# Stick-breaking heads with queries on the partitions, and half-width recurrence levels, in a two-block transformer kernel

## The chip, the core and the metric

The kernel runs on one core of a Trainium2 chip, in one launch. The metric is the device time of an execution in microseconds (us). The median of three runs before the change is 1744.52 us (1741.60 to 1746.47). Engines are written as in the profile: PE (TensorE), DVE (VectorE), ACT (ScalarE), POOL (GpSimd), SP (the engine that issues most DMAs).

## The reference, cut to what matters

512 tokens of width 1024 in fp32 pass through two blocks. The first has a sparse attention, a gating unit and a mixture of experts; the change doesn't touch it. The second puts 16 meta tokens in front of the sequence and mixes it in two ways: eight stick-breaking heads of dimension 64 and four recurrent heads of dimension 128. An output projection and a second mixture of experts follow. The stick-breaking heads compute, for a query t and a key s:

```python
z = jnp.einsum('bhtd,bhsd->bhts', q[:, :, t0:t1], k[:, :, :t1]).astype(jnp.float32) * scale
valid = (s_pos < t_pos) & (s_pos >= LEAD_PAD)
log_beta = jax.nn.log_sigmoid(z)
log_keep = jnp.where(valid, jax.nn.log_sigmoid(-z), 0.0)
log_tail = lax.cumsum(log_keep, axis=3, reverse=True) - log_keep
w = jnp.where(valid, jnp.exp(log_beta + log_tail), 0.0)
outs.append(jnp.einsum('bhts,bhsd->bhtd', w.astype(v.dtype), v[:, :, :t1]))
```

With softplus(z) = max(z, 0) + ln(1 + exp(-|z|)), the weight is exp(z - R), where R is the sum of softplus(z) over the keys from s to t - 1. The recurrent heads, in chunks of 128 tokens, are

```python
bc = jnp.cumsum(gc, axis=2)
diff = bc[:, :, :, None, :] - bc[:, :, None, :, :]
decay = jnp.exp(jnp.where(causal, diff, -jnp.inf))
scores = jnp.einsum('bhtd,bhsd,bhtsd->bhts', qc, kc, decay)
o = jnp.einsum('bhts,bhsv->bhtv', scores, vc) + jnp.einsum('bhtd,bhdv->bhtv', qc * jnp.exp(bc), state)
```

## The kernel before

**The stage.** The work around the change is the mixer loop of the second block: `for i in range(TURNS): for place in range(PLACES):`, written once for each engine. TURNS is 10, PLACES is 4. Turn i starts the scores of stick-breaking head i; the later parts of a head follow in the next turns. From turn 1 to 7 each of the four places also holds one step of the recurrent heads (`step_after`), 28 steps in all, seven levels for each of four heads. Each engine works its own list in order and waits on semaphores for the others; nothing is scheduled at run time. The order is written out by hand.

**A stick-breaking head** keeps keys on the partitions and queries along the row. The five key blocks (one of meta tokens, four of 128 tokens) have 512, 512, 384, 256 and 128 queries, `STICK` = 1792 columns. PE makes the scores z (`scores`, L1961). DVE copies them from PSUM to the buffer `zw` (profile names: arena), scaled and with the causal mask (`stick_scores`, L2721 to L2725). ACT takes |z|, exp(-|z|) and the logarithm into `sps` (ring or misc; L2273, L2275, L2280). DVE adds max(z, 0) (`stick_logits`, L2738, 1792 columns). POOL sums whole blocks of keys (`sums_of_blocks`, L2967, four additions). PE makes the sums R over keys, which lie on the partitions, by products with triangles of ones (`sums_behind`, L1969 and L1972). DVE subtracts them from z (`stick_subtract`, L2734). ACT exponentiates (`stick_weights`, L2284), PE multiplies with the values (`stick_out`, L1982, 14 products), ACT copies the output (L2288), POOL and DVE square, sum and norm it (`head_square` L2952, `head_sums` L2708, `head_norm` L2946, L2947, L2958).

**A recurrence step.** At level lv the queries of the later half of each group of P >> lv tokens meet the keys of the earlier half. POOL makes the differences of decays (`level_diff`, L2982 and L2984), ACT exponentiates (L2294), DVE multiplies queries and keys (`level_products`, L2745 and L2750), PE makes the level's scores (L2012, four products with 128 queries each), and DVE copies them under a mask into `hsc` (`level_read`, L2768, 512 columns). Only the 256 queries of the later halves carry anything.

PSUM has eight banks of 512 fp32 columns. Five go round among the stick-breaking units, three among the recurrent ones (`second_block_units`); PE waits before it fills a bank until its last reader is done. After the loop come the transposes of the mixed rows (`mixed_turned`, L1887), their split in a high and a low part (L2324, L2810) and the output projection (`out_product`, L1727). Its last weight tiles are loaded by SP into the three ring buffers, which lend space to the loop (`sps`, `qexp`, `kd`, `kdR`, `states`).

## Time and profile before

| | us |
|---|---|
| median of 3 runs | 1744.52 |
| profiled execution | 1751.0 |
| its span | 1749.3 |
| PE busy in the span | 1599.1 (91%) |
| DVE | 820.0 (47%) |
| ACT | 335.7 (19%) |
| POOL | 240.2 (14%) |

The profiled execution took 1751.0 us: the span from its first to its last instruction, and 1.7 around it. Busy times are averages over stages of very different kind. In the first block and in both expert stages DVE and POOL are mostly idle; the mixer loop, from about 1027 to 1193 us, is where four engines work at once.

### The profile page before, as it was taken

How to read it: one execution, taken by the hardware profiler on the slowest of the kernel's cores; microseconds unless marked ns; L12 is line 12 of the kernel's file. 1: busy time of each engine (PE TensorE's matmuls, PEld its weight loads, DVE VectorE, ACT ScalarE, POOL GpSimd, SP SyncE). 2: the span in 40 equal slices, each digit the busy share in tenths (PEclk: the TensorE clock that was granted, in tenths of full speed). 3: DMA queues.
4: the chain of work that ended last, by engine and by line, in shares of the span. 5: the costliest groups of instructions: out<-in, count | busy, mean ns of one | idle time of the engine just before them, and what ended most of it. 6: DMA issues, size and time to landing. Idle time of an engine off the chain costs nothing.

```text
span 1749.3 us, 18915 instructions
## 1 busy us (share of the span) xinstructions
PE 1599.1 (91%) x7674; PEld 1027.3 (59%) x7674; DVE 820.0 (47%) x1360; ACT 335.7 (19%) x574; POOL 240.2 (14%) x298
## 2 busy tenths in 40 slices
PE   7999999999999697788699979999699998999996
PEld 5688888877888332333488866778543333333332
DVE  6898645537374410111742358985533322323232
ACT  3422000027101110111311154541200000101011
POOL 1100003300000311100300024781120000000000
PEclk9999999999999899999799988999799999999998
DMA  5122222220237899999322200015899999999993
GB/s 202 49 96 97 74 97 94 97 81 16 101 140 287 331 380 425 428 427 395 156 96 86 90 19 1 1 49 222 312 341 430 430 429 427 430 430 429 430 430 164
DMA packets 52927, 403.26 MB, mean 231 GB/s; under 512 B 13648, under 2 KB 15056, under 8 KB 23776
## 3 DMA queue, kind: packets, MB, share of 16 engines
q1 hardware_dynamic: 45408, 389.34, 55.3%
q0 software_dynamic: 7424, 12.61, 2.1%
q8 instruction: 65, 1.06, 0.2%
q14 instruction: 30, 0.25, 0.0%
HBM read 397.69 MB, written 16.81 MB: 237 GB/s over the span
## 4 chain that ended last, share of the span: by engine, by line
PE 71%; DMA 16%; DVE 6%; issue 3%; ACT 3%; POOL 2%; SPq 0%; POOLq 0%; DVEq 0%; ACTq 0%
PE bank L1727 37%; PE bank L738 14%; DMA arena<-in_expert_in 6%; PE bank L753 6%; PE bank L717 2%; DMA ring<-in_expert_up 2%; DMA arena<-in_expert_up 2%; DMA arena<-in_expert_gate 2%; DMA ring<-in_expert_gate 2%; DMA arena<-in_expert_out 2%; PE bank L916 1%; PE bank L1719 1%; PE bank L718 1%; PE bank L1838 1%; PE bank L1854 1%
## 5 line engine op out<-in xcount | busy, mean ns | idle before, releaser
L738 PE MATMUL bank<-arena 128*64 128x512 f32 x960 | 276.0, 621 | 26.4 <-DMA arena<-in_expert_in 10.7
L738 PE MATMUL bank<-ring,arena 128*64 128x512 f32 x576 | 183.6, 621 | 9.0 <-DMA ring<-in_expert_in 4.7
L738 PEld LDWEIGHTS bank<-arena 128*64 128x64 f32 x960 | 84.1, 142 | 179.2 <-issue 176.7
L1122 DVE TENSOR_TENSOR resid<-resid,bank 128x512 f32<-128x512 f32 x120 | 80.7, 685 | 202.1 <-PE bank L718 202.1
L2411 DVE CAST ring_high<-ring 128x2048 fp32r<-128x2048 f32 x51 | 62.7, 1229 | 236.9 <-DMA ring<-in_stream_a 145.7
L2412 DVE TENSOR_TENSOR ring_low<-ring,ring_high 128x2048 fp32r<-128x2048 f32 x60 | 138.7, 2312 | 6.3 <-ACT ring_high L2083 4.3
L753 PE MATMUL bank<-arena 128*64 128x512 f32 x448 | 114.4, 595 | 13.8 <-DVE arena L1147 6.5
L1727 PE MATMUL bank<-ring_low,xn_high 128*128 128x512 f32 x288 | 113.0, 392 | 0.3 <-DVE ring_low L2412 0.3
L1727 PE MATMUL bank<-ring_high,xn_high 128*128 128x512 f32 x288 | 112.2, 390 | 0.0
L1727 PE MATMUL bank<-ring_high,xn_low 128*128 128x512 f32 x288 | 112.1, 389 | 0.0
L738 PEld LDWEIGHTS bank<-ring,arena 128*64 128x64 f32 x576 | 55.6, 142 | 66.7 <-issue 66.7
L1143 DVE TENSOR_TENSOR arena<-misc,bank 128x256 f32<-128x256 f32 (+1 forms) x32 | 17.6, 551 | 158.8 <-ACT misc L1028 135.6
L1229 POOL DMA_INDIRECT arena<-xn_rows,token_table x32 | 32.6, 1019 | 416.7 <-PE bank L916 379.6
L753 PE MATMUL bank<-ring,arena 128*64 128x512 f32 x288 | 78.6, 596 | 7.1 <-issue 3.7
L753 PEld LDWEIGHTS bank<-arena 128*64 128x64 f32 x448 | 39.4, 137 | 75.5 <-issue 73.1
L1727 PE MATMUL bank<-xn_low,ring_high 128*128 128x512 f32 x192 | 75.0, 391 | 2.4 <-DVE misc L2547 2.4
L1727 PE MATMUL bank<-xn_high,ring_high 128*128 128x512 f32 x192 | 74.8, 389 | 0.0
L1727 PE MATMUL bank<-xn_high,ring_low 128*128 128x512 f32 x192 | 74.7, 389 | 0.0
L1028 ACT ACTIVATE misc<-bank 128x256 f32<-128x256 f32 (+1 forms) x32 | 15.7, 490 | 294.5 <-PE bank L738 294.5
L1261 POOL TENSOR_SCALAR rstd<-ssq 128x1 f32<-128x1 f32 x25 | 11.0, 442 | 422.0 <-ACT arena L1351 258.9
L1114 DVE SCALAR_TENSOR_TENSOR y_low<-bank,gate_slot,y_high 128x512 fp32r<-128x512 f32 x32 | 24.0, 751 | 91.9 <-ACT y_high L1042 91.9
L717 PEld LDWEIGHTS bank<-y_high,spread 128*128 128x128 f32 x128 | 24.0, 187 | 71.9 <-issue 69.2
(393 smaller groups left out, 3052.9 us busy)
## 6 DMA issues: line engine op xcount, KB each, us to landing
ring<-in_stream_a SPq DMA_DIRECT2D x42, 1024.0 KB, 5.0
arena<-in_expert_gate SPq DMA_DIRECT2D x20, 2048.0 KB, 23.0
arena<-in_expert_in SPq DMA_DIRECT2D x18, 2048.0 KB, 33.8
arena<-in_expert_up SPq DMA_DIRECT2D x18, 2048.0 KB, 24.3
arena<-in_expert_down SPq DMA_DIRECT2D x18, 2048.0 KB, 24.5
ring<-in_expert_up SPq DMA_DIRECT2D x12, 2048.0 KB, 25.1
ring<-in_expert_down SPq DMA_DIRECT2D x12, 2048.0 KB, 24.7
ring<-in_expert_gate SPq DMA_DIRECT2D x12, 2048.0 KB, 24.2
```

The costliest lines, as they stand in the source:

```text
L717: nc.tensor.matmul(bank[bank_at][:, :], w, half_of(y_high[:, p % 2, :], half), start=first, stop=False)
L718: ins = nc.tensor.matmul(bank[bank_at][:, :], w, half_of(y_low[p % 2], half), start=False, stop=last)
L738: last = nc.tensor.matmul(h[side * SLOTS:(side + 1) * SLOTS, :], tokens[:, k, side * SLOTS:(side + 1) * SLOTS], w[:, k * 512:(k + 1) * 512 ...
L753: last = nc.tensor.matmul(bank[6 + n][side * SLOTS:(side + 1) * SLOTS, :], hidden[:, f, side * SLOTS:(side + 1) * SLOTS], w[:, f * D + n * ...
L916: last = nc.tensor.transpose(bank[k // 4][:, k % 4 * P:(k % 4 + 1) * P], m.xg[:, p % XG, k * P:(k + 1) * P], c("ident"))
L1114: V.scalar_tensor_tensor(half_of(y_low[p % 2], half), bank[6 + half][:, :], gate_slot[:, p:p + 1], half_of(y_high[:, p % 2, :], half).bitc ...
L1122: nc.vector.tensor_tensor(place, place, bank[bank_at][:, :], ALU.add).then_inc(m.moe_added, 1)
L1143: V.tensor_tensor(m.act[:, 0:m.width], m.sg[:, 0:m.width], up_of(m), ALU.mult).then_inc(m.act_ready, 1)
L1229: G.indirect_dma_start(m.xg[:, p % XG, :], None, m.xn_rows[:, :], bass.IndirectOffsetOnAxis(ap=m.token_table[:, p:p + 1], axis=0), bounds_ ...
L1727: ins = nc.tensor.matmul(b, left(k)[l_], right(k)[r_], start=(first and k == 0 and i == 0), stop=(last and k == KC // 2 - 1 and i == 2))
L2411: then(V.tensor_copy(hi, ring_raw[n % RING]))
L2412: V.tensor_tensor(lo, ring_raw[n % RING], hi.bitcast(F32), ALU.subtract).then_inc(weights_split, 1)
```

## The change

Queries move to the partitions, keys along the row. A head has, for each query block t, the 128 keys of its own block (four pieces, 512 columns) and the rest in front of it: 16 meta keys and t whole blocks, `REST_W` = 16, 144, 272, 400 columns. `STICK` falls from 1792 to 1344, as 112 padding rows of the meta block are gone. The sums R now run along a row, so DVE makes them with eight reversed scans (`stick_sums`): four over the own blocks, which start at zero, then four over the rests, which start from the result of the own block. The scan adds both ln(1 + exp(-|z|)) and max(z, 0), which ACT writes to `above_zero` (a fourth pass, Relu). POOL makes z - R in one subtraction (`exponents`). PE transposes it in 14 pieces, ACT exponentiates from PSUM into `w_turned`, and PE multiplies with the values as before, the meta part with 16 rows. ACT copies the rest's scores out of PSUM, DVE the own blocks' with the mask.

The loop has 9 turns instead of 10. Head i's scans stand at place 2 of turn i, its subtraction at place 3, its transposes at place 1 of the next turn, exponentials at 2, outputs at 3. At each level, the 256 queries are written side by side; PE takes 64 of them in a product, and DVE copies 256 columns. `w_turned` lies in ring buffer 1, so SP's last but one half tile waits for the last output. The turn order of the transposes at the end is new.

```diff
-    put("strict", np.where(row < col, 0.0, NEG))
+    put("strict", np.where(col < row, 0.0, NEG))
@@ sizes
-FIRST_T = [max(s, 1) - 1 for s in range(NT2)]
-STICK_W = [SEQ - P * f for f in FIRST_T]
+REST_W = [META + t * P for t in range(NT)]
+REST_AT = [SEQ + sum(REST_W[:t]) for t in range(NT)]
+STICK = SEQ + sum(REST_W)
+SCORE_UNITS = ((), (0, 1, 2), (3,))
+TURNED_UNITS = (((0, 0), (0, 1), (0, 2), (0, 3)), ((1, 1), (1, 2), (1, 3), (3, 3)), ((2, 2), (2, 3)))
-TURNS = SBH + 2
+TURNS = SBH + 1
-TURN_ORDER = (4, 5, 6, 7, 0, 1, 2, 3)
+TURN_ORDER = (4, 5, 0, 1, 2, 6, 7, 3)
@@ buffers and SP
-        zw = [at(arena, i * STICK, [STICK]) for i in range(3)]
+        zw = [at(arena, i * STICK, [STICK]) for i in (2, 3)]
+        above_zero = at(arena, STICK, [STICK])
+        w_turned = at(ring[1], 0, [TURNED])
-                    sp.wait_ge(psum_filled2, U2.filled(("R", SBH - 2, NT2 - 1)))
+                    sp.wait_ge(psum_filled2, U2.filled(("WT", SBH - 2, 3)))
+                if n == first + 2 * len(STREAM2) - 2:
+                    sp.wait_ge(psum_filled2, U2.filled(("SO", SBH - 1)))
@@ PE
-            def sums_behind(g, blocks):
-                pe.wait_ge(sums_ready, g + 1)
...
+            def exponents_turned(g):
+                pe.wait_ge(exponents_ready, g + 1)
+                e = zw[g % 2]
+                for j, unit in enumerate(TURNED_UNITS):
+                    b = begin2(("WT", g, j))
+                    for n, (s, t) in enumerate(unit):
+                        a = t * P if s == t else REST_AT[t] + META + s * P
+                        last_ = nc.tensor.transpose(b[:, n * P:(n + 1) * P], e[:, a:a + P], c("ident"))
+                    end2(last_)
...
-                    last_ = nc.tensor.matmul(b[:, t * P:(t + 1) * P], keys_,
-                                             qE[:, n % 2, t * P:(t + 1) * P], start=True, stop=True)
+                    last_ = nc.tensor.matmul(b[:, t * P // 2:(t + 1) * P // 2], keys_,
+                                             qE[:, n % 2, t * P // 2:(t + 1) * P // 2], start=True, stop=True)
...
-                    if sums_blocks(i, place):
-                        sums_behind(i - 1, sums_blocks(i, place))
-                    if place == 2 and i >= 2:
-                        stick_out(i - 2)
+                    if place == 3 and i >= 1:
+                        stick_out(i - 1)
                     if step_after(i, place) is not None:
                         step(step_after(i, place))
+                    if place == 1 and i >= 1:
+                        exponents_turned(i - 1)
@@ ACT
+            def stick_scores(h):
+                if h >= 2:
+                    act.wait_ge(psum_filled2, U2.filled(("WT", h - 2, 3)))
+                for j in (1, 2):
...
+                    read2(A.activation(zw[h % 2][:, a:end], b[:, 0:end - a], ACT.Copy, scale=SBD ** -0.5))
...
+                A.activation(above_zero, zw[h % 2], ACT.Relu).then_inc(log_ready, 1)
                 act.wait_ge(act_step, 2 * h + 2)
                 A.activation(v, v, ACT.Ln, bias=1.0).then_inc(log_ready, 1)
...
             def stick_weights(g):
-                wait_read2(act, ("R", g, NT2 - 1))
-                A.activation(zw[g % 3], zw[g % 3], ACT.Exp).then_inc(weight_ready, 1)
+                for j, unit in enumerate(TURNED_UNITS):
+                    b, w = unit2(("WT", g, j)), P * len(unit)
+                    read2(A.activation(w_turned[:, SEQ * j:SEQ * j + w], b[:, 0:w], ACT.Exp))
+                b = unit2(("WT", g, 3))
+                read2(A.activation(w_turned[0:META, META_AT:META_AT + SEQ], b[0:META, :], ACT.Exp))
@@ DVE
+            def sums_from_last(v, a, w, initial):
+                part = v[:, a:a + w][:, ::-1]
+                return V.tensor_tensor_scan(part, part, above_zero[:, a:a + w][:, ::-1], initial, ALU.add, ALU.add)
+            def stick_sums(h):
+                v = sps[h % 2]
+                dve.wait_ge(log_ready, 2 * h + 2)
+                for t in range(NT):
+                    ins = sums_from_last(v, t * P, P, 0.0)
+                then(ins)
+                for t in range(NT):
+                    ins = sums_from_last(v, REST_AT[t], REST_W[t], v[:, t * P:t * P + 1])
+                ins.then_inc(sums_ready, 1)
...
-                read_state(V.copy_predicated(s, level_mask(lv).bitcast(U32),
-                                             b[:, :].rearrange("p (t q) -> p t q", q=P)))
+                read_state(V.copy_predicated(later_queries(hsc[:, h % 2, :], lv), later_mask(lv).bitcast(U32),
+                                             compact_level(b[:, 0:SEQ // 2], lv)))
@@ POOL
-            def sums_of_blocks(g):
...
+            def exponents(g):
+                pool.wait_ge(sums_ready, g + 1)
+                G.tensor_tensor(zw[g % 2], zw[g % 2], sps[g % 2], ALU.subtract).then_inc(exponents_ready, 1)
```

**How the order moves.** PE in turn 6, from the step that follows its scores, before (L1969 and L1972 are the block sums, L1887 and L2005 open a recurrent head, L2012 is a level product, L1982 the outputs of a head):

```order
L2012 MATMUL bank<-resid,arena 128x128 x4
L1969 MATMUL bank<-misc,cst 128x512
L1972 MATMUL bank<-misc,cst 128x512
L1969 MATMUL bank<-misc,cst 128x512
L1972 MATMUL bank<-misc,cst 128x384
L1887 MATMUL bank<-cst,ring 128x128 x4
L2005 MATMUL bank<-arena 128x128 x4
L2012 MATMUL bank<-resid 128x128 x4
L1982 MATMUL bank<-arena 128x64 x14
L2012 MATMUL bank<-resid 128x128 x4
```

The same place after (L2029 is the level product, L1983 and L1987 the transposes):

```order
L2029 MATMUL bank<-resid,arena 128x64 x4
L1889 MATMUL bank<-cst,ring 128x128 x4
L2022 MATMUL bank<-arena 128x128 x4
L2029 MATMUL bank<-resid 128x64 x4
L1983 MATMUL bank<-cst,arena 128x128 x10
L1987 MATMUL bank<-cst,arena 16x128 x4
L2029 MATMUL bank<-resid 128x64 x4
```

Block sums no longer stand between the level products; transposes stand there, and the outputs move one place back.

DVE at place 2 of a turn, before (L2738 is the addition of max(z, 0)):

```order
L2745 TENSOR_TENSOR resid<-resid,arena 128x4x64
L2750 TENSOR_TENSOR resid<-resid,arena 128x4x64
L2768 COPY_PREDICATED resid<-cst,bank 128x512
L2738 SCALAR_TENSOR_TENSOR ring<-arena,ring 128x1792
L2745 TENSOR_TENSOR resid<-resid,arena 128x8x32
L2750 TENSOR_TENSOR resid<-resid,arena 128x8x32
```

And after (L2758 are the scans, listed under the name that the build gives them):

```order
L2775 TENSOR_TENSOR resid<-resid,arena 128x256
L2780 TENSOR_TENSOR resid<-resid,arena 128x4x64
L2811 COPY_PREDICATED resid<-cst,bank 128x256
L2758 SCALAR_TENSOR_TENSOR ring<-ring,arena 128x128 x4
L2758 SCALAR_TENSOR_TENSOR ring<-ring,arena 128x16
L2758 SCALAR_TENSOR_TENSOR ring<-ring,arena 128x144
L2758 SCALAR_TENSOR_TENSOR ring<-ring,arena 128x272
L2758 SCALAR_TENSOR_TENSOR ring<-ring,arena 128x400
L2775 TENSOR_TENSOR resid<-resid,arena 128x256
L2780 TENSOR_TENSOR resid<-resid,arena 128x8x32
```

Eight scans stand in the place of one addition, in front of the next step's products.

## Rows read from the trace of the kernel before

**Rows 1.** Windows: length, then busy of PE, PEld, DVE, ACT, POOL; clock; DMA.

```profile
1026.90:1192.60 165.70, 149.69 (x845) 115.24 (x845) 140.03 (x266) 90.37 (x114) 105.27 (x131) 0.92 0.07 26
...
1103.90:1165.20 61.30, 60.25 (x359) 46.62 (x359) 55.91 (x106) 32.65 (x40) 52.91 (x64) 1.00 0.00 1
...
1192.60:1237.00 44.40, 44.40 (x199) 36.74 (x200) 20.83 (x22) 4.76 (x9) 2.85 (x7) 1.00 0.60 241
```

**Rows 2.** PE timeline at the turns and the end: start, length, instruction.

```profile
1060.64 3.31 PE L1961 MATMUL bank<-arena 64*128 64x512 f32 x10
...
1080.97 6.34 PE L1961 MATMUL bank<-arena 64*128 64x512 f32 x10
...
1103.87 3.28 PE L1961 MATMUL bank<-arena 64*128 64x512 f32 x10
...
1173.98 1.06 PE L2012 MATMUL bank<-resid,arena 128*128 128x128 f32 x8
...
1192.58 0.50 PE L1727 MATMUL bank<-ring_low,state_high 128*128 128x512 f32 x1 [0.52 <-DVE state_low L2810]
```

**Rows 3.** DVE and POOL timelines where they meet, and five scans alone.

```profile
1045.87 3.63 DVE L2702 TENSOR_TENSOR_SCAN arena<-cst,arena 128x128 f32<-128x128 f32 x5
...
1043.61 3.86 POOL L2967 TENSOR_TENSOR ring<-ring 128x128 f32<-128x128 f32 x4 [3.41 <-DVE ring L2738]
...
1056.12 2.02 DVE L2738 SCALAR_TENSOR_TENSOR misc<-arena,misc 128x1792 f32<-128x1792 f32 x1
...
1056.21 2.41 POOL L2984 TENSOR_TENSOR resid<-arena 128x256 f32<-128x256 f32 x1
...
1090.12 1.69 DVE L2702 TENSOR_TENSOR_SCAN arena<-cst,arena 128x128 f32<-128x128 f32 x5
```

**Rows 4.** Groups of instructions: busy us, mean ns; idle before, releaser.

```profile
L2768 DVE COPY_PREDICATED resid<-cst,bank 128x512 f32<-128x512 uint32 x28 | 20.4, 730 | 0.9 <-PE bank L2012 0.8
...
L2734 DVE TENSOR_TENSOR arena<-arena,bank 128x512 f32<-128x512 f32 (+3 forms) x40 | 19.5, 523 | 8.9 <-PE bank L1972 8.0 <-DVE resid L2768 0.3 <-PE bank L1961 0.2
...
L2284 ACT ACTIVATE arena<-arena 128x1792 f32<-128x1792 f32 x8 | 13.5, 1686 | 8.7 <-DVE arena L2734 8.7
...
L2967 POOL TENSOR_TENSOR misc<-misc 128x512 f32<-128x512 f32 x4 | 5.1, 1270 | 0.3
...
L3000 POOL TENSOR_TENSOR arena<-arena 128x512 f32<-128x512 f32 x3 | 4.5, 1491 | 0.2
```

**Rows 5.** PE timeline in turn 4, and transposes at the end.

```profile
1108.07 1.02 PE L1969 MATMUL bank<-misc,cst 128*128 128x512 f32 x2
...
1111.29 1.05 PE L2012 MATMUL bank<-resid,arena 128*128 128x128 f32 x8
1112.18 3.24 PE L1982 MATMUL bank<-arena 128*128 128x64 f32 x28
...
1118.06 0.81 PE L1969 MATMUL bank<-misc,cst 128*128 128x384 f32 x2
...
1190.15 1.92 PE L1887 MATMUL bank<-cst,arena 128*128 128x128 f32 x16
```

**Rows 6.** DVE and POOL timelines of turn 5: free instructions.

```profile
1134.53 0.42 DVE L2745 TENSOR_TENSOR resid<-resid,arena 128x256 f32<-128x256 f32 x1
1134.86 0.42 DVE L2750 TENSOR_TENSOR resid<-resid,arena 128x256 f32<-128x256 f32 x1
...
1135.36 0.61 POOL L2982 TENSOR_TENSOR resid<-arena 128x256 f32<-128x256 f32 x1 [4.36 <-DVE resid L2750]
...
1139.91 3.75 POOL L2967 TENSOR_TENSOR misc<-misc 128x128 f32<-128x128 f32 x4
```

**Rows 7.** Windows around a fall of PE's clock, columns as in rows 1.

```profile
1076.00:1080.00 4.00, 1.65 (x14) 1.48 (x14) 3.85 (x6) 0.58 (x1) 3.77 (x4) 1.00 0.00 0
1080.00:1084.00 4.00, 4.00 (x12) 2.32 (x13) 3.93 (x8) 2.22 (x2) 3.43 (x6) 0.62 0.00 0
1084.00:1088.00 4.00, 4.00 (x10) 2.46 (x10) 2.92 (x9) 0.27 (x1) 0.00 (x0) 0.50 0.00 0
```

220 lines of the change are left out of this document (108 added, 112 removed).

## The prediction

> **What bounds the kernel now.** I read the windows first, to find the stage that the diff touches, then the PE timeline for the rhythm of that stage, then DVE and POOL side by side at the places where an instruction took longer than its shape asks for.
>
> The change lives in the mixer loop of the second block. It runs from PE's scores of head 0 at 1026.9 us to the start of the output projection at 1192.58 [rows 1, 2]. That is 165.7 us of a span of 1749.3; in it PE is busy 149.7, DVE 140.0, POOL 105.3 and ACT 90.4 us [rows 1]. Nothing in front of the loop changes in length. Behind it the projection runs at 44.4 busy of 44.4 us [rows 1], and the expert stage starts from it, so I let a gain or a loss of the loop pass to the end one to one.
>
> Turns are marked by PE's score products: turns 2, 3 and 4 start at 1060.64, 1080.97 and 1103.87, and the last level product, the end of turn 7, begins at 1173.98 [rows 2] and takes 0.89. From 1103.87 to 1174.87 four turns take 71.0 us, 17.75 each. In 1103.9 to 1165.2 PE is busy 60.25 of 61.30, DVE 55.91 and POOL 52.91 [rows 1]. So PE is full, but two engines stand close behind, and they aren't independent. POOL's 256-wide subtraction takes 0.61 us when free (L2982) [rows 6] and 2.41 beside DVE's 2.02 us L2738 (L2984); it ends at 1058.62, 0.5 after DVE's [rows 3]. The five scans L2702 take 1.69 us alone and 3.63 beside POOL's adds L2967 [rows 3]. DVE instructions with two operands in SBUF and POOL's instructions exclude each other. DVE work on a PSUM operand does not: L2768 averages 730 ns over all 28 [rows 4]. I call what the two engines share "the pair". The Trainium skill, SBUF — State Buffer, "Who interferes with whom", states this as an exclusive lock, and the trace agrees. That rule speaks against this change: sums that leave PE land where two engines already wait for each other.
>
> **PE, part by part.** The four block sums from 1108.07 to 1111.29 have 1920 moving columns in 3.22 us, 1.68 ns a column, so a product with 512 advances PE by 0.86 us, one with 128 columns by 0.2225 (four L2012 from 1111.29 to 1112.18, 0.89) [rows 5]. Removed per head: the block sums L1969 and L1972, 3072 columns in nine products, 5.2 us: the four above and five more from 1118.06, at least 1.9 in proportion and 2.0 with the small ones at 0.22 [rows 5]. The scores take 3.2 now (3.28 with the drain) [rows 2]; after, four of 128 columns (0.89) and four of 16, 144, 272 and 400 columns (0.22 + 0.24 + 0.45 + 0.67 = 1.58), 2.47. Added: 14 transposes; 16 took 1.92 us [rows 5], so 1.6. The output products stay 14, at 3.1 (28 records, 3.24 with the drain) [rows 5]. Net 4.3 us per head, 35 in all.
>
> The level products go from 128 to 64 moving columns with the same 128-column weights. L1982 has just that shape: 28 records, 14 products, in 3.1 us, 0.22 each against 0.2225 [rows 5]. I count nothing. The Trainium skill, TensorE: Matmul & The Clock Gate, "Back-to-back issue gap", gives an isolated gap of the columns over 2.4 GHz plus 2.5 ns, by which 112 products would shed about half, some 12 us; the same section notes that the spacing of a load and product pair is set by both, and the row sides with that.
>
> **DVE.** Removed per head: L2738 (2.02), five subtractions (19.5 us over eight heads, 2.4 each [rows 4]) and seven of eight score copies, which read PSUM. Added: one score copy of 512 and eight scans over 1344 columns. A free scan of 128 takes 1.69 / 5 = 0.34 [rows 3]; in proportion 1344 take 3.55, and part of the 0.34 is paid per instruction, so the four long ones are cheaper: 3.4. The copies under a mask, 28 of 512 columns at 0.73 [rows 4], go to 256: about 0.5, 6 us in all. All of this but L2738 and the scans is outside the pair.
>
> **The pair.** Here little is removed. Before, per head: L2738 1.95 and four adds on POOL, 3.75 from first to last [rows 6], together 5.7. After: scans 3.4 and one POOL subtraction of 1344. POOL's add of 512 takes 1.27 [rows 4]; in proportion 1344 take 3.3, with a fixed part less; the slowest row, L3000 with 1.49 [rows 4], gives 3.9, and 2.6 is the low end (1.0 for 512). I take 3.0. Together 6.4, 0.7 more. The rest of the pair in a mean turn: 7.4 level differences on POOL at 0.6 = 4.4 [rows 6]; square and norm of a stick head 1.2; three passes of 512 for three heads over seven turns, 1.4; 7.4 level products on DVE, which start 0.33 apart [rows 6] = 2.5; L2789 and L2791, 512 columns each, 0.6 for half a head. That is 10.1, so 15.8 before and 16.5 after, against a turn of 17.75. Today PE's 17.4 (98%) is longest; after, PE needs 13.1 and the pair 16.5 plus hand-overs, for each waits in order behind the other. If the 1.95 us that a turn lasts beyond the pair's 15.8 stayed, a turn would be 18.4; if they vanished, 16.5. I take 17.8, no change, and keep -1.2 to +0.7 per turn over seven turns, -8 to +5 us.
>
> ACT gets longer but has room: 32.65 busy of 61.30 [rows 1]. Passes of 1792 (1.69, L2284 [rows 4]) become 1.3 at 1344, four instead of three; two score copies of about 0.5 and four weight exponentials read from PSUM, some 2.0, against one of 1.69. About +1.7 per turn. Its chain is hidden as long as the logarithms are done before DVE reaches the scans, two places later; if that cover is gone, a turn is late by what is missing, up to 1.3. Queued behind a scan that waits is DVE's next level product, and PE's level behind that; queued behind the 1344-wide subtraction is the next level difference, then ACT's exponential.
>
> **Slow stretch.** Before the clock fell at 1080.9, PE was busy 1.65 of 4.00 us; it then ran at the half-rate level, 0.62 and 0.50 in the next two stretches, at full busy [rows 7]. That turn took 22.9 (1080.97 to 1103.87) where the turn before, with the same scans L2702, took 20.3 [rows 2]: 2.6 to 3.4 us too many. After, PE's 13.1 us plus some 5 for such a stretch is 18, inside that turn, so the stretch no longer costs: -3. But PE will idle a quarter of each turn and the clock will fall more often; where it falls, each level product is 0.9 us later in DVE's chain. I charge +1 in all, net -2.
>
> **The end.** From the last level product's end to the projection: 1174.87 to 1192.58 = 17.7 us [rows 2]. In it stand head 7's block sums, subtraction, one 1.7 us exponential, the outputs of two heads (3.07 each) and 16 transposes on PE. After, one turn is gone and two heads' outputs become one: POOL's norm of the last but one state head (two passes like L3000 and a root, 3.7) and subtraction (3.0), 1.6 transposes, 2.0 exponentials, 3.07 outputs, copy and square 1.1, low part 0.75, some 15.2 from the last DVE product, which lies about 1 us before that end: 14.2. -3.5, bounds -6 and 0. SP loads the third of the last four half tiles now behind head 7's output instead of earlier. The projection needs it half of 44.4 us after its start, so it stays hidden; were it late, every us counts.
>
> Turns 0 and 1: a longer first ACT chain against cheaper sums: 0, bounds +-3.
>
> **Sum.** 0 - 2 - 3.5 = -5.5. The profiled execution took 1751.0 (span 1749.3 and 1.7 around) and would take 1745.5. It lies 6.5 above the median 1744.5, so on that scale the change gives 1739.
>
> **Rivals.**
> A, PE alone is the bound, and what DVE and POOL lose to each other hides behind it. For it: PE 98% busy. A turn falls to PE's 13.1 at about 92% busy, 14.3, so 3.4 us less in each of seven turns, 24, and little at the end: 1720. Against: rows 3, and POOL busy 52.91 of 61.30 [rows 1]. Chance 0.16.
> B, slower through the clock. The same loop with PE at the half-rate level needs 2 x 13.1 = 26.2 us of PE in a turn. If a stretch like rows 7 comes in each turn, and the levels wait for PE there, each turn loses about 2 us: +14 less 3.5 at the end, 1755; if it stayed low, +60. It decides from the point at which slow stretches fill more than about 40% of the loop. For it: 1.65 of 4.00 us busy sufficed. Against: outputs and scores fill most gaps. Chance 0.16.
> C, the scans or the subtraction dearer (columns read backwards; an initial value from SBUF): every 1 ns a column is 1.3 us of the pair per head, +11 in all, 1750. Chance 0.10.
> D, my case, 0.58.
> The Trainium skill, DVE: opcode table, instruction layouts, handler registers and perf-mode slots, "Datapath and trigger behaviour", says that the built-in scan runs at half throughput. The trace agrees: 2.6 ns a column for 128 against 1.13 in L2738 [rows 3].
>
> **Numbers.** What this kernel's measurement can tell from no change is 0.3%, 5.2 us. D spans 1729 to 1749: 0.30 faster, 0.25 same, 0.03 slower. A is faster. B gives 0.15 slower, 0.01 same. C 0.06 slower, 0.04 same. Together faster 0.46, same 0.30, slower 0.24. Range 1724 to 1757.
>
> **What would show it.** Right: turns of 17 to 18.5 us with PE busy about three quarters; POOL's 1344-wide subtraction at 2.6 to 3.3 us and scans of 3.4 per head, both longer where they meet; 14 us from the last level product to the projection; level products still 0.22 us apart. Wrong: turns under 16 us (A); the granted clock low in over 40% of the loop and PE busy again (B); free scans over 0.45 us for 128 columns (C); a wait of the projection for a weight tile.

## The result, and the profile after

The changed kernel takes 1778.09 us (median of 4 runs, 1773.32 to 1778.46) against 1743.33 of the kernel before on the same chip: ratio 1.0178, 95% interval [1.0152, 1.0205]. That is slower; the forecast was 1739, range 1724 to 1757. The profiled execution has a span of 1776.7 us against 1749.3. The profiled execution of the kernel before (1751.0 us) lies 7.7 above its median, so the traces can account for 27.4 of the 34.8 us between the medians.

The windows of the mixer loop (scores of head 0 to projection, whole), of two stretches in it and of its end; columns as in [rows 1]:

```profile
1028.91:1219.48 190.57, 161.25 (x861) 143.16 (x860) 121.42 (x228) 100.00 (x162) 93.83 (x107) 0.69 0.03 8
1106.00:1121.60 15.60, 15.60 (x63) 13.76 (x63) 6.38 (x12) 6.45 (x9) 7.36 (x11) 0.50 0.00 0
1149.10:1169.40 20.30, 20.30 (x83) 17.99 (x83) 8.59 (x17) 7.99 (x11) 12.65 (x16) 0.50 0.00 1
1203.70:1219.48 15.78, 13.30 (x88) 11.30 (x87) 9.55 (x15) 7.10 (x13) 5.38 (x8) 0.82 0.09 24
```

The loop takes 190.6 us against 165.7 [rows 1]. DVE and POOL did shrink (DVE 121.4 for 140.0, POOL 93.8 for 105.3), yet PE is busy 161.3 us for 149.7, with less work. The reason stands in the third column from the end: the mean granted clock of the loop is 0.69, not 0.92. Since the clock has only two levels (0.50 is 1.2 GHz, 1.00 is 2.4), 62% of the loop ran at the low one (2 x 0.31), against 16% before. In the second and third row PE is busy all through, at 0.50.

The PE timeline at the turns (score products of heads 2 and 7, the last level product, the projection), as [rows 2]:

```profile
1063.46 5.16 PE L1963 MATMUL bank<-arena 64*128 64x128 f32 x16
...
1181.88 5.22 PE L1963 MATMUL bank<-arena 64*128 64x128 f32 x16
...
1201.96 1.97 PE L2029 MATMUL bank<-resid,arena 128*128 128x64 f32 x8
...
1219.48 0.79 PE L1729 MATMUL bank<-ring_low,state_high 128*128 128x512 f32 x1 [1.56 <-DVE state_low L2853]
```

From the start of turn 2 to the end of the last level product: 1063.46 to 1203.7, 140.3 us; before, 1060.64 to 1174.87, 114.2 [rows 2]. The six turns went from 19.0 to 23.4 us each and carry nearly the whole loss, 26.0. Turns 0 and 1 take 34.5 for 33.8 us, the end 15.8 for 17.7, and the loop starts 2.1 us later. 26.0 + 0.7 - 1.9 + 2.1 = 26.9 of the 27.4 us between the spans.

How PE runs in such a turn: the output stage (L1997 with 128 rows, L1999 with 16) at either clock, and the wait ahead of it:

```profile
1058.29 0.33 PE L1997 MATMUL bank<-arena,ring 128*128 128x64 f32 x2
1058.55 0.43 PE L1999 MATMUL bank<-arena,ring 16*128 16x64 f32 x2
1058.91 0.66 PE L1997 MATMUL bank<-arena,ring 128*128 128x64 f32 x4
...
1062.43 1.10 PE L2029 MATMUL bank<-resid 128*128 128x64 f32 x8
...
1076.96 0.49 PE L1997 MATMUL bank<-arena,ring 128*128 128x64 f32 x2 [1.53 <-ACT ring L2317]
1077.37 0.68 PE L1999 MATMUL bank<-arena,ring 16*128 16x64 f32 x2
...
1084.25 1.11 PE L1889 MATMUL bank<-cst,ring 128*128 128x128 f32 x4
...
1101.62 0.69 PE L1997 MATMUL bank<-arena,ring 128*128 128x64 f32 x2 [3.76 <-ACT ring L2317]
```

(Two records are one fp32 product.) At the full clock the stage takes 1058.29 to 1062.43, 4.14 us, not the 3.07 of the same 14 products before: a 16-row product (1058.55 to 1058.91) advances PE by 0.36 us where a 128-row one takes 0.22, and the two 128-row products behind it take 0.59 (1058.91 to 1059.50), not 0.44. So it is the change between the two kinds that costs, some 0.15 us each (an estimate: 1.07 us over seven changes). At the low clock the stage is 7.29 us (1076.96 to 1084.25). The scores take 5.2 us at the low clock, in the turns shown above, and 2.7 at the full one (1088.08 to 1090.76, for 2.47 in the forecast).

What came before the clock fell: windows around three falls in the changed kernel, to set beside [rows 7], columns as in [rows 1]:

```profile
1060.10:1063.50 3.40, 3.40 (x27) 3.07 (x26) 3.12 (x9) 1.08 (x3) 1.97 (x3) 1.00 0.00 0
1063.60:1067.00 3.40, 3.40 (x14) 3.25 (x15) 3.37 (x4) 0.00 (x0) 2.70 (x3) 0.50 0.00 0
...
1125.00:1128.40 3.40, 3.40 (x25) 3.00 (x25) 3.33 (x7) 0.70 (x2) 1.15 (x2) 1.00 0.02 5
1128.40:1131.80 3.40, 3.40 (x16) 3.17 (x16) 3.40 (x2) 0.37 (x1) 3.25 (x2) 0.50 0.00 0
...
1172.80:1176.10 3.30, 3.30 (x25) 2.90 (x23) 2.91 (x6) 1.11 (x2) 1.98 (x3) 1.00 0.00 0
1176.20:1179.60 3.40, 3.40 (x17) 3.17 (x15) 0.00 (x0) 0.90 (x2) 3.40 (x3) 0.50 0.02 5
```

Each time PE was busy all through a stretch at 1.00, and the next was granted 0.50. What stood ahead of these falls were, for the most part, the 64-column and 16-row products of the output stage. But they are not the rule. The record of the clock has ten falls in this loop; the 3.4 us ahead of the other seven:

```profile
1032.85:1036.25 3.40, 0.29 (x1) 0.00 (x0) 3.29 (x7) 3.31 (x5) 2.52 (x4) 1.00 0.00 0
1049.92:1053.32 3.40, 1.92 (x18) 1.78 (x18) 3.34 (x4) 2.68 (x5) 3.40 (x5) 1.00 0.00 0
1073.81:1077.21 3.40, 1.87 (x17) 1.66 (x15) 2.57 (x8) 3.40 (x7) 2.67 (x5) 1.00 0.02 5
1097.70:1101.10 3.40, 0.16 (x2) 0.02 (x1) 3.21 (x9) 3.40 (x10) 2.59 (x4) 1.00 0.00 0
1142.08:1145.48 3.40, 1.12 (x9) 0.97 (x8) 2.31 (x5) 3.40 (x5) 0.89 (x3) 1.00 0.00 0
1193.28:1196.68 3.40, 2.36 (x18) 2.08 (x16) 3.25 (x6) 2.10 (x6) 3.19 (x3) 1.00 0.60 176
1213.76:1217.16 3.40, 3.40 (x25) 3.00 (x25) 2.96 (x5) 0.14 (x2) 1.80 (x2) 1.00 0.00 0
```

Six of the ten came while PE idled for part of the time, as in [rows 7], where it was busy 1.65 of 4.00 us. The low stretches behind these six add up to 81.9 us, the two longest (20.5 and 23.9 us) among them; those behind the four fully busy ones to 36.4 us of the loop. So both roads lead down. Once the clock was low, PE busy all through did not bring it back for 15.6 and 20.3 us (the first rows of this section). The kernel before has two falls in its loop and 27.3 us at the low clock, against 118.4.

The groups that answer to [rows 4], within the loop and by shape:

```profile
L1999 PE MATMUL bank<-arena,ring 16*128 16x64 f32 x64 | 18.1, 374 | 0.0
...
L2811 DVE COPY_PREDICATED resid<-cst,bank 128x256 f32<-128x256 uint32 x28 | 14.6, 520 | 35.2 <-PE bank L2029 35.1
...
L3005 POOL TENSOR_TENSOR arena<-arena,ring 128x1344 f32<-128x1344 f32 x4 | 14.3, 3576 | 9.6 <-DVE ring L2758 9.6
...
L3005 POOL TENSOR_TENSOR arena<-arena,misc 128x1344 f32<-128x1344 f32 x4 | 12.6, 3140 | 2.2 <-DVE misc L2758 2.2
```

The first head's eight scans on the DVE timeline, which answer to the five of [rows 3]:

```profile
1042.69 3.69 DVE L2758 TENSOR_TENSOR_SCAN ring<-ring,arena 128x128 f32<-128x128 f32 x8 [5.76 <-ACT ring L2310]
```

The copy under the mask has fallen from 730 to 520 ns, but DVE waited 35.1 us for PE's level products ahead of it; before, such waits came to 0.8 [rows 4]. DVE waits for PE now.

### The profile page after: what moved, and what is told of

Same layout as the page of the kernel before. It is cut to its first block, busy times and chain, and to the rows that moved or that the text cites. A ratio compares the mean times of both kernels' runs of the same rounds, so it can differ in the third digit from the quotient of the medians.

```text
span 1776.7 us, 18931 instructions
## 1 busy us (share of the span) xinstructions
PE 1614.4 (91%) x7690; PEld 1054.9 (59%) x7690; DVE 799.2 (45%) x1320; ACT 344.8 (19%) x622; POOL 228.5 (13%) x274
## 4 chain that ended last, share of the span: by engine, by line
PE 77%; DMA 12%; ACT 4%; DVE 3%; issue 2%; POOL 1%; SPq 0%; POOLq 0%; ACTq 0%; DVEq 0%
PE bank L1729 38%; PE bank L736 15%; PE bank L751 7%; DMA arena<-in_expert_in 6%; PE bank L715 2%; PE bank L1997 2%; DMA ring<-in_expert_up 2%; DMA arena<-in_expert_up 2%; DMA arena<-in_expert_out 2%; PE bank L1963 1%; PE bank L914 1%; PE bank L716 1%; PE bank L1721 1%; PE bank L2029 1%; PE bank L1840 1%
## 5 line engine op out<-in xcount | busy, mean ns | idle before, releaser
L1120 DVE TENSOR_TENSOR resid<-resid,bank 128x512 f32<-128x512 f32 x120 | 80.7, 685 | 199.8 <-PE bank L716 199.8
## 6 DMA issues: line engine op xcount, KB each, us to landing
arena<-in_expert_in SPq DMA_DIRECT2D x18, 2048.0 KB, 33.8
ring<-in_expert_up SPq DMA_DIRECT2D x12, 2048.0 KB, 23.4
```

Source lines behind the costliest of these rows:

```text
L1120: nc.vector.tensor_tensor(place, place, bank[bank_at][:, :], ALU.add).then_inc(m.moe_added, 1)
```

## The experiments

The theories: 1, the granted clock falls because wide products were taken out and narrow ones left (1b: because TensorE idles, whatever the width of its products); 2, the chain through VectorE, GpSimd and ScalarE is itself longer and the clock only goes along; 3, the switches between 128-row and 16-row products make TensorE the bound; 4, the order ties TensorE and ScalarE into a cycle.

Eighteen kernels were run. "Loop" is the profiled execution's time from the first scores to the projection, "clock" the mean granted clock in it, "PE" its busy time there; loop, clock and PE are each of one execution. Each ratio is taken against executions of the kernel before in the same round, whose median went from 1743.3 to 1747.0.

| kernel | median us | ratio to before [95%] | loop us | clock | PE us |
|---|---|---|---|---|---|
| before | 1743.3 | | 165.8 | 0.92 | 149.8 |
| changed | 1778.1 | 1.0178 [1.0152, 1.0205] | 190.6 | 0.69 | 161.3 |
| half_levels_alone | 1748.4 | 1.0017 [1.0001, 1.0033] | 164.5 | 0.92 | 149.0 |
| full_levels | 1774.6 | 1.0176 [1.0158, 1.0195] | 190.7 | 0.71 | 158.0 |
| sums_cut | (below) | | 163.5 | 0.77 | 138.5 |
| filler | 1786.0 | 1.0235 [1.0212, 1.0257] | 199.8 | 0.85 | 183.0 |
| wide_columns | 1769.3 | 1.0152 [1.0133, 1.0172] | 184.2 | 0.78 | 149.2 |
| wide_filled | 1760.4 | 1.0075 [1.0048, 1.0103] | 176.4 | 0.88 | 149.1 |
| outputs_later | 1798.8 | 1.0318 [1.0276, 1.0359] | 212.4 | 0.63 | 176.6 |
| meta_paired | 1762.2 | 1.0121 [1.0064, 1.0177] | 178.4 | 0.73 | 147.8 |
| scores_ahead | 1775.6 | 1.0190 [1.0155, 1.0225] | 189.1 | 0.68 | 163.3 |
| ahead_paired | 1768.1 | 1.0144 [1.0107, 1.0182] | 181.4 | 0.71 | 154.1 |
| ahead_wide_paired | 1758.6 | 1.0067 [1.0035, 1.0098] | 174.2 | 0.80 | 139.2 |
| ahead_wide_paired_filled | 1748.8 | 1.0025 [0.9999, 1.0051] | 166.7 | 0.89 | 136.5 |
| filled_narrow | 1754.9 | 1.0063 [1.0041, 1.0084] | 174.1 | 0.86 | 142.4 |
| wide_paired_filled | 1749.4 | 1.0031 [1.0012, 1.0050] | 163.7 | 0.92 | 132.0 |
| ahead_filled_start | 1756.3 | 1.0069 [1.0048, 1.0091] | 175.9 | 0.88 | 155.7 |
| before_start_filled | 1747.2 | 1.0013 [0.9995, 1.0031] | 165.4 | 0.95 | 156.3 |
| rows_full | 1757.4 | 1.0058 [1.0033, 1.0082] | 171.3 | 0.74 | 140.2 |
| rows_wide_filled | 1740.6 | 0.9966 [0.9952, 0.9981] | 158.0 | 0.92 | 124.0 |

### Which part of the change: half_levels_alone, full_levels

```
half_levels_alone, on the kernel before (also the compact copy under the mask):
-  matmul(b[:, t*P:(t+1)*P], keys_, qE[:, n%2, t*P:(t+1)*P])
+  matmul(b[:, t*P//2:(t+1)*P//2], keys_, qE[:, n%2, t*P//2:(t+1)*P//2])
full_levels: the reverse of it, on the changed kernel
```

> The kernel before with only the second part of the change: levels multiply and copy the later halves' 256 queries. Theory 1 (clock): the block sums' wide products are still there, so the clock stays as before, and the shorter predicated copies give back 0 to 5 us: 1738-1745; if the 64-column level products alone were what lowers the clock, 1755 or more. Theory 2: 1736-1742.

> The changed kernel with one of its two parts taken back: recurrence levels multiply and copy all 512 queries again. Theory 1 (clock): 128 columns in place of 64 in 112 products raise TensorE's activity a little, and the predicated copy costs 28 x 0.3 us on VectorE: 1765-1785. Theory 2: the copies only add to VectorE, 1783-1790.

Alone, the half-width levels measured 1.0017 [1.0001, 1.0033], no gain: DVE's busy time in the loop fell by 4.3 us and the loop by 1.3. Taken back from the changed kernel they moved nothing either (1.0176 against 1.0178). Neither run finds the loss in the half-width levels, so it is that of the rebuilt stick heads.

### Are the removed wide products what held the clock: sums_cut

```
on the kernel before, for each of 5 blocks:
-  matmul(b[:, 0:w], tri_ge, sps[:, a:a+w]); matmul(b[:, w-behind:w], tri_lt, sps[:, a+w:a+w+behind])
+  matmul(b[:, 0:64], tri_ge, sps[:, a:a+64])
-  zs - b[:, 0:w]
+  zs - b[:, 0:64] broadcast to w
```

> The kernel before with its block sums on TensorE cut from 9 wide products to 5 of 64 columns for each head (work left out: only the first 64 columns of each block are summed, VectorE subtracts these for the whole block at the same width, so its instructions keep their size). Some 4.2 us of TensorE work less in each turn, nothing else changed. Theory 1 (clock: the wide products kept the granted clock up): low time in the loop rises from 27 us to 60 or more, and the time does not fall by more than 5 us, more likely rises: 1740-1765. Theory 2 (chain): the clock doesn't matter, TensorE was not the bound: 1735-1743, turns of 17-18 us as before.

Its whole time (2136.1 us) can't be compared, for with other numbers out of the mixer the expert stage behind it has other work; the loop can. There some 33 us of PE work at the full clock (5.2 less 5 x 0.22 for each of 8 heads) are gone, and no work of the other engines with it; the granted clock fell from 0.92 to 0.77 (75 us low for 27) and the loop from 165.8 only to 163.5. This is the change's first step by itself. In its profiled execution every one of its six falls came behind a stretch in which PE idled (busy 0.00 to 2.70 of 3.4 us): with the sums gone PE had more to wait for, and that brings the clock down without any new narrow products. How much the low clock took back isn't shown: a turn of this kernel with the clock at 1.00 all through (1076.41 to 1093.81) took 17.4 us, near the 17.75 of before, with DVE busy 16.8 of it, which suggests that the other engines would have kept most of the gain in any case.

### Width and filling: filler, wide_columns, wide_filled

```
filler, ahead of each of 28 waits for level_ready (56 products):
+  matmul(b[:, :], ident, sbq[:, 0, :]) x2
wide_columns:
-  matmul(b[:, t*64:(t+1)*64], ..., sbv[:, s+1, g*64:(g+1)*64])
+  matmul(b[:, t*128:(t+1)*128], ..., sbv[:, s+1, g//2*128:(g//2+1)*128])    (copy takes 64 of 128)
-  matmul(b[:, t*64:t*64+64], keys_, qE[..., t*64:t*64+64])
+  wide = 128 if t < 3 else 64; matmul(b[:, t*64:t*64+wide], keys_, qE[..., t*64:t*64+wide])
wide_filled: wide_columns, 2 extra products at the outputs' wait, 1 at every third level's
```

> The changed kernel with two extra products of 512 columns (unused, overwritten by the level product behind them) placed ahead of each of the 28 waits for a level's operands, 56 in all. Theory 1 (the clock): the loop is long because TensorE is granted the low level for over half of it; work put where it only waited keeps the granted clock up, turns shrink from 22.5-24.5 us to 18-19, and the time falls from 1778 to 1735-1750 although work was added. Theory 2 (the chain through VectorE, GpSimd and ScalarE is itself longer, and the low clock only goes along with the waits): the clock may rise, the turns stay at 22-24 us, and the time stays at 1775-1790.

> The changed kernel with the moving side of its narrow products made 128 columns: all 14 output products of a stick head (the neighbour head's 64 columns are computed too and not copied), and three of four in each level product (the next tile's 64 columns, written over by the next product). No product more, none less; by the rows of before 64 and 128 columns take about the same 0.22 us. Theory 1 (clock, and it is the narrow products that don't hold it): fewer low stretches, 1745-1765. Theory 1b (clock, but idle TensorE lowers it, whatever the width): no change, 1770-1780, low stretches as before. Theory 2 (longer chain on the other engines): no change, 1775-1780.

> The kernel with 128-column output and level products (wide_columns) with 21 extra products of 512 columns, only where TensorE was seen to wait: two ahead of the wait for each head's turned weights (heads 0 to 6), one ahead of the level product at the third place of each of 7 turns. That is 18 us of work at the full clock. Theory 1 (clock): 56 extra products were too many (TensorE was busy 183 of 200 us); 21 keep the clock and fit into the idle 35 us of wide_columns: low time in the loop from 82 to under 40 us, loop from 184 to 165-175 us, 1748-1760. Theory 2 (chain through the other engines): the loop stays at 182-190, 1767-1775.

The filler raised the clock to 0.85, as the clock theory says, but did not lower the time: 48 us of extra work went onto a PE that then was busy 183 of 200 us. My number for it was wrong, as 56 products don't fit the waits, and its 1786 us lies in the range of theory 2, so this run does not decide. Of its eight falls seven came with PE busy 3.29 to 3.40 of the 3.4 us ahead: with the waits filled, the falls behind idle PE are nearly gone, those behind busy PE are not.

Widening adds no product; the clock went to 0.78, PE's busy time from 161.3 to 149.2 and the loop from 190.6 to 184.2. Its five falls all came behind idle PE:

```profile
1030.57:1033.97 3.40, 0.36 (x2) 0.00 (x0) 3.29 (x7) 3.31 (x5) 2.45 (x4) 1.00 0.00 0
1068.12:1071.52 3.40, 1.67 (x14) 1.20 (x11) 2.62 (x8) 3.40 (x5) 1.97 (x4) 1.00 0.02 5
1095.42:1098.82 3.40, 0.00 (x0) 0.00 (x0) 3.37 (x8) 3.40 (x9) 2.22 (x4) 1.00 0.00 0
1136.38:1139.78 3.40, 1.23 (x12) 0.88 (x10) 2.70 (x8) 3.40 (x9) 0.00 (x0) 1.00 0.00 0
1184.17:1187.57 3.40, 1.29 (x8) 1.05 (x8) 3.29 (x6) 2.06 (x6) 3.15 (x3) 1.00 0.41 173
```

It isn't free: at the full clock the output stage takes 4.67 us (1055.82 to 1060.49 in its PE timeline) for 4.14. Its 1769.3 us lies between the two forecasts (1745 to 1765, and 1770 to 1780), and its ratio (1.0152) overlaps the changed kernel's interval; with 21 fillers it is apart from it: 1.0075 [1.0048, 1.0103], clock 0.88. That speaks against theory 2, which had 1767 to 1775. The forecasts of theory 1 (loop 165 to 175, 1748 to 1760) were just missed.

### The order of outputs and scores: outputs_later, scores_ahead, ahead_paired, ahead_wide_paired, ahead_wide_paired_filled, wide_paired_filled

```
outputs_later:  stick_out(i-1) behind step() at place 3, not ahead of it
scores_ahead:   -  place 0: scores(i)
                +  place 3 of turn i-1: scores(i), ahead of stick_out(i-2); ScalarE's score copies with it
*_paired:       the 16-row product comes first in tiles 1 and 3, last in tiles 0 and 2
*_wide:         as wide_columns;   *_filled: 1 extra product at the outputs' wait and at every third level
```

> The changed kernel with one swap in the order: the output products of a stick head stand behind the level product at the fourth place of a turn, not ahead of it. Theory 1 (clock): TensorE waits 2.5-3.8 us less for ScalarE's exponentials in each turn, but the level product then waits as long for its own operands; the low stretches remain, 1770-1778. Theory 2 (the wait for the turned weights sits in the loop's cycle): the levels no longer stand behind it, turns shorten by 1-2 us, 1763-1770.

> The changed kernel with the score products of the next stick head (and ScalarE's copies of them) moved from the start of a turn to the fourth place of the turn before, ahead of the output products. Theory 4 (a cycle between two engines): in the changed kernel the next scores stand behind the outputs on TensorE, the outputs wait for ScalarE's exponentials of the turned logits, and these stand behind ScalarE's passes over the current scores; the path is about 10.1 us of ScalarE plus 8.5 us of TensorE at the full clock (14.7 at the low one), so 18.6 to 24.8 us a turn. With the scores ahead of the outputs it is broken: turns of 18-20 us, 1742-1758. Theory 1 (the clock alone): the same products in another order, 1770-1780.

Theory 4 came from this stretch of the chain of waits of wide_filled, where every span of ACT's passes ends in PE's outputs and every span of outputs and scores in ACT's passes:

```profile
1096.67 0.53 ACT resid L2332
1097.19 1.22 ACT arena L2313
1098.41 1.21 ACT misc L2315
...
1101.93 1.23 ACT ring L2320 x3
1103.16 0.47 ACT ring L2322
1103.63 0.04 issue
1103.67 0.49 PE bank L1999 x2
...
1108.41 1.03 PE bank L2034 x8
1109.45 2.69 PE bank L1963 x16
```

> scores_ahead with the 16-row products side by side in pairs, as in meta_paired (which measured 1762). Theory 4: both add, 2 to 8 us below scores_ahead. Theory 1: as meta_paired alone, 1760-1765.

> ahead_paired with the 128-column output and level products of wide_columns (the neighbour's columns are computed and not used). Theories 1 and 4 together: the cycle is broken and the granted clock stays up more: low time under 60 us, 1732-1748. Theory 4 alone: the clock no longer matters once the cycle is broken, equal to ahead_paired. Theory 1 alone: 1755-1762.

> The kernel ahead_wide_paired with 14 extra products of 512 columns where TensorE waited: one ahead of the wait for each head's turned weights (heads 0 to 6), one ahead of the level product at the third place of each of 7 turns; 12 us of TensorE work. Theories 1 and 4: the clock stays up in nearly all of the loop, and the 12 us fit into waits: 1730-1745. If the loop is bound by TensorE once the cycle is broken, the 12 us come on top: 1745-1755.

> The kernel ahead_wide_paired_filled with the order of the changed kernel: scores back at the start of the turn, behind the outputs. Theory 4 in its weaker form (the cycle TensorE outputs, scores, ScalarE's passes, exponentials, outputs is 18.6-20 us at the full clock and binds only once the clock is up; at the low clock TensorE binds anyway, which is why scores_ahead alone did nothing): turns of 20 us or more, 1757-1765. Without such a cycle: 1746-1752, as with the scores ahead.

Theory 4 fell. With the scores ahead the time stayed (1.0190 against 1.0178), and the weaker form, that the cycle binds once the clock is up, fell too: with the scores in the order of the change wide_paired_filled is as fast as with them ahead (1.0031 and 1.0025, intervals that overlap), and its turns at the full clock are 18.0 to 19.8 us, not 20 or more. The chain had shown what ended last, not what a reordering would give. What moved the time in this series was pairing (ahead_paired), then width, then filling, with the clock at 0.71, 0.80 and 0.89; the intervals are apart at the step to width alone and overlap at the other two. outputs_later was a surprise: one swap, one more wait before the scores, +21 us, and the lowest clock of all, 0.63. I had expected no loss. Whether the longer chain or the clock that fell with it costs more there is not separated.

In the profiled execution of wide_paired_filled the loop has the mean clock of before, 0.92, and takes 163.7 us against 165.8. That execution is the fastest of its twelve, and the one of the kernel before is slower than its median, so the pair of loops flatters the change; by all executions this kernel is 0.3% slower than before. The twelve tell more by themselves: the same program took 1742.7 us with a mean clock over the whole execution of 0.962 and 1757.9 with 0.953, and the ten between lie in this order but for 0.001 of clock.

### Rows: meta_paired, rows_full, rows_wide_filled

```
meta_paired: as *_paired above
rows_full:
-  matmul(out_, w_turned[0:16, ...], sbv[0:16, 0, ...])
+  matmul(out_, w_turned[:, ...], sbv[:, 0, ...])      (16 transposed columns become 128; sbv rows 16.. are zero)
rows_wide_filled: rows_full + wide_columns + the 14 fillers of *_filled
```

> The changed kernel with the 16-row products of neighbouring query tiles put side by side (last of tile 0, first of tile 1, and so on), so that a head's output stage switches 4 times between 128-row and 16-row products and not 7. In the trace of the changed kernel each switch costs about 0.14 us at the full clock. Theory 1 (clock): TensorE saves 0.4 us a head at the full and 0.8 at the low level, 1772-1778. Theory 3 (the switches are what makes TensorE the bound): 1765-1772.

> The changed kernel with its 16-row products (the four meta-token products of each head's output stage and their transposes) made 128-row products: the transposes take 128 columns, and the value rows behind the 16 meta tokens are zeroed, so the result stays the same. As many products. It tells why pairing the 16-row products (meta_paired) brought 16 us, more than the 3.4 us of its saved switches. If the switch between 128 and 16 rows is a cost of its own and few rows also fail to hold the clock: the output stage at the full clock is 3.1-3.3 us, not 4.14, low time in the loop under 96 us, 1755-1765. If the rows don't matter: 1775-1780.

> The kernel wide_paired_filled (1749.4; its profiled execution had the low clock for 27 us of the loop, which took 163.7 us) with the 128-row products of rows_full in place of the pairing. Theory 1: the output stage shrinks by another 0.3-0.6 us a head and the clock holds a little better, 1740-1748, no slower than before. If the low stretches come anyway: 1749-1755.

meta_paired came out at 1762.2 us, below both its forecasts (1772 to 1778, and 1765 to 1772). Its output stage takes 3.63 us at the full clock, for 4.14. Two 16-row products side by side:

```profile
1056.68 0.65 PE L1997 MATMUL bank<-arena,ring 16*128 16x64 f32 x4
1057.27 1.33 PE L2003 MATMUL bank<-arena,ring 128*128 128x64 f32 x10
```

They advance PE by 0.59 us, twice 0.22 and one change of 0.15.

The output stage of rows_full at the full clock, on the PE timeline:

```profile
1056.78 0.33 PE L1997 MATMUL bank<-arena,ring 128*128 128x64 f32 x2
1056.94 0.39 PE L1999 MATMUL bank<-arena,ring 128*128 128x64 f32 x2
...
1059.85 1.06 PE L2029 MATMUL bank<-resid 128*128 128x64 f32 x8
```

1056.78 to 1059.85 is 3.07 us, the forecast's figure, with eight times the rows in the four products. The whole kernel falls from 1778.1 to 1757.4 us, 21 us, and the ratios are far apart (1.0178 [1.0152, 1.0205], 1.0058 [1.0033, 1.0082]). The 1.07 us a head come to 8.6; the loop gave 19.2, with the clock at 0.74 for 0.69. Part of that is the stage itself at the low clock: all eight output stages took 46.9 us in the changed kernel and take 34.9 here. The other 7 us go with the rest. The low time in the loop is 89 us for 118, and none of the seven falls came behind a fully busy stretch (at most 2.50 of 3.4 us), though the outputs still have 64 columns. So the changes between 128 and 16 rows, theory 3, are part of the loss.

The last kernel is the only one below the kernel before, by 0.3%: 0.9966 [0.9952, 0.9981], 1740.6 us. Loop windows of rows_full and of rows_wide_filled, columns as in [rows 1]:

```profile
1027.14:1198.48 171.34, 140.16 (x861) 130.38 (x861) 123.99 (x228) 100.39 (x162) 94.48 (x107) 0.74 0.03 8
```

```profile
1027.61:1185.57 157.96, 123.95 (x889) 107.34 (x888) 127.13 (x228) 100.76 (x162) 95.03 (x107) 0.92 0.03 9
```

It computes what the changed kernel does, with 14 products more, and PE is busy 37 us less in the loop (161.3 to 124.0). Turn 2 to the end of the last level product takes 1061.65 to 1172.0, 110.4 us or 18.4 a turn. It has three falls, none behind a fully busy stretch, and 24 us at the low clock.

### What holds the clock, and what a low stretch costs: filled_narrow, before_start_filled, ahead_filled_start

```
filled_narrow, on ahead_wide_paired_filled:
-  matmul(b[:, :], ident, sbq[:, 0, :])
+  matmul(b[:, 0:64], ident, sbq[:, 0, 0:64]) x4
before_start_filled: 5 products of 512 columns ahead of the first kd_ready, 5 ahead of the first sums_ready
ahead_filled_start: 14 such ahead of the first kd_ready, on ahead_wide_paired_filled
```

> The kernel ahead_wide_paired_filled (1748.8, low clock in 37.5 of 167 us of the loop) with each of its 14 extra 512-column products replaced by 4 products of 64 columns at the same place: about the same TensorE time (4 x 0.22 for 0.85 us), an eighth of the columns in each, half of them in all. Theory 1 in its narrow form (only the columns that pass keep the clock, not that TensorE is busy): low time 50-75 us as without extra products, 1754-1760. Theory 1b (any busy TensorE holds the clock): 35-45 us low, 1747-1751.

> The kernel before with 10 extra products of 512 columns in its two first waits of 5 us (5 ahead of the first head's turned keys, 5 ahead of the first block sums). Theory 1: the low stretch of 17 us at its loop's start goes, worth 2-6 us, 1738-1742. Other theories: no change, 1743-1746.

> The kernel ahead_wide_paired_filled with 14 more extra products of 512 columns in the 13.9 us in which TensorE waits for the first head's operands at the start of the loop. Theory 1: the clock, low for 20 us from there, stays up in the first two turns, 2 to 6 us: 1742-1747, for the first time no slower than before. If the first turns are bound elsewhere: 1748-1751.

Narrow fillers of the same PE time did less: 1.0063 [1.0041, 1.0084] against 1.0025 [0.9999, 1.0051], loop 174.1 against 166.7. Against no filler (ahead_wide_paired: 1.0067, 174.2 us, clock 0.80) they raised the clock to 0.86 and gave no time. That leans to the narrow form of theory 1, but the intervals meet, and the low time fell to 47.8 us, less than this form expected. How much columns and how much mere busy time count stays open.

before_start_filled kept the clock up at its loop's start (mean 0.95 for 0.92), and the time didn't move (1.0013 [0.9995, 1.0031]; forecast 1738 to 1742). ahead_filled_start was expected at 1742 to 1747 and took 1756.3: the low stretch at the start shrank from 20.5 to 3.4 us, but 37.5 us of low clock came later in the loop, for 17.1, and the mean clock was no higher (0.88). Why is open. So the low stretch at the start, where PE waits for others, cost nothing that these runs show. What a low microsecond costs where the others wait for PE is not isolated; as PE does half its work in it, half a microsecond at most (an estimate).

## Why the prediction was wrong

**The step that failed** is "Slow stretch", the -2 us of the sum. It saw rightly that "PE will idle a quarter of each turn and the clock will fall more often", and charged "+1 in all" for it. That size was the error: the low clock went from 27.3 to 118.4 us of the loop (16% to 62%), in stretches of up to 23.9 us, and six turns grew by 26.0 us. It also knew only one road, idle PE. Six of the ten falls are of that kind; four came with PE busy all through, behind the narrow products of the output stage, and PE stayed at 0.50 through a fully busy stretch of 20.3 us. Nothing in the prediction asked what brings the clock back. Rival B had the sign, the idle PE and the point from which it decides ("over 40% of the loop and PE busy again"), but prices for two other cases (+14 less 3.5 for a stretch in each turn, +60 for all of the loop); measured was +35, and I had given it 0.16. sums_cut shows the fall of the clock from the removal alone. rows_wide_filled, with the clock at 0.92 and the 16-row products made whole, takes 1740.6 us with the same algorithm, close to the forecast of 1739; but with its fuller products and its fillers it is not the kernel that the forecast was for.

**Outputs, "stay 14, at 3.1".** Wrong by 1.07 us a head at the full clock, for I took the 16-row products as equal to the rest. rows_full puts it right: 3.07.

**The turn at 17.8.** Measured 23.4. With rows and clock mended 18.4 over six turns (19.0 before on the same marks), and 18.0 over the four from 1100.09, where the forecast had read its 17.75, with 12 us of extra PE work in the loop. Nothing speaks against the term for the pair, but it was no longer what bound the changed kernel, whose PE was busy 161.3 of 190.6 us.

**PE's 13.1 us a turn.** With 35 us less than 149.7 the loop would have had 115 us of PE work. rows_wide_filled has 124.0 busy at the same mean clock of 0.92, and 112 without its fillers: about right as work, useless without the clock.

**Level products at 64 columns cost as much as at 128.** Right within 0.05 us: in the changed kernel's PE timeline four start at 1093.54 and the next instruction at 1094.38, 0.84 for 0.89; half_levels_alone shows no gain.

**DVE and POOL.** Scans 3.69 us for 3.4 per head; subtraction 3.14 and 3.58 on average for 3.0 (bounds 2.6 and 3.9); copies under the mask 0.52 for 0.5. All near, so rival C isn't the cause.

**The end at 14.2.** 15.8 us at a mean clock of 0.82; at the full clock (rows_wide_filled, 1172.0 to 1185.57) 13.5. Right but for the clock.

**The start at 0.** +0.7, inside the bounds.

**Rival A** (PE alone binds, 1720) fell: in sums_cut a lighter PE alone shortened the loop by 2.3 us.

**The exclusion of DVE and POOL** was read rightly but could not decide: waits for PE, 35.1 us, had taken its place.

The Trainium skill, TensorE: Matmul & The Clock Gate, "PE-mode transpose", says that transposes don't count as busy for the clock gate in the way that other products do. The change adds 14 of them to a head, a rule against it that the prediction didn't weigh; no run here takes the transposes apart from the rest. The same page of the Trainium skill, "Why this matters for your kernels", says that a single product with 32 rows takes the time of one with 128. The traces agree for the product itself, here with 16 rows: two side by side take 0.59 us, one change of 0.15 included. What they add is the change: where the two kinds alternate it is 0.36 against 0.22 us.

**Left open.** How the loss divides between the falls behind idle PE and those behind narrow products; what share of the gain from rows_full to rows_wide_filled (16.8 us) is width and what fillers; and why pairing alone (meta_paired) brought 16 us of median with an interval as wide as [1.0064, 1.0177].

## What to carry to other kernels

When a change takes wide products off TensorE and leaves it narrow ones, read the granted clock of the stage as a term of its own: ask not only whether the engine idles but what its busy time is made of, and price the stage at both levels before trusting any sum of durations. An experiment that removes the work and leaves the rest tells this in one run. Products with few rows among full ones can be made full ones with zero rows, and that made the stage shorter (3.07 us for 4.14). A neighbour's columns made it longer, by 0.53 us beside 16-row products and by 0.06 beside full ones (3.13), and still paid through the clock when fillers came with them.

## What the runs showed that was not expected

- The granted clock fell from 2.4 to 1.2 GHz not only behind idle PE (six of ten falls) but also behind stretches in which PE was busy 3.40 of 3.40 us, mostly with 64-column and 16-row fp32 products (four of ten). With 128 columns or 128 rows in their place no fall came behind a fully busy stretch (wide_columns, rows_full; one execution each).
- A 16-row product among 128-row ones advances PE by 0.36 us at the full clock and one with 128 rows by 0.22; a head's 14 products take 4.14 and 3.07 us. The cost is that of the change, about 0.15 us each.
- Some 33 us of PE work removed from the loop gave 2.3 us (sums_cut), while 14 products of 512 columns added gave 10 us (1758.6 to 1748.8, intervals that overlap a little).
- The time of one and the same kernel goes with its clock: wide_paired_filled ran from 1742.7 us (mean clock 0.962) to 1757.9 us (0.953) in 12 runs.
